# Scores of a step stand behind the values of the step two ahead, in an attention and MLP stack on one core

## The chip, the core and the metric

The program runs on one core of a Trainium2 chip. Its time is the device time in us of that core. Before the change it took 1929.63 us (median of three runs, 1927.41 to 1931.17). TensorE (PE in the rows) multiplies matrices, VectorE (DVE), ScalarE (ACT) and GpSimd (POOL) do elementwise work, and SyncE (SP) issues most DMAs. Each engine takes its own instructions in the order in which they are written and waits at semaphores for the others.

## The reference

256 tokens of width 1024 go through four layers of a first block and two layers of a second block.

```
first block, for each of 4 layers:
    q, k, v (and more) = x @ w_in
    mix = dsa | dilated | moba attention (by layer: 0 and 3, 1, 2)
    mo  = memory attention, 4 heads
    x = layer_norm(ALPHA * x + concat(mix, mo) @ w_out)
    x = layer_norm(ALPHA * x + (silu(x @ w_gate) * (x @ w_up)) @ w_down)
second block, for each of 2 layers:
    u = rms_norm(x) @ w_in
    differential, latent (MLA) and sliding window attention, each gated and projected
    x = x + rms_norm(y @ w_out);  x = x + sigmoid(x @ w_ple_gate) * (p @ w_ple_proj)
```

Every attention is scores, mask, softmax, values, in float32.

## The kernel before

**Weights.** Each weight matrix comes in units of two 128-row tiles by up to 512 columns. SP loads a unit into `raw` (ten slots), ScalarE rounds it to `w_hi` (L1205, eight slots), GpSimd makes the rest `w_lo` (L1177), and TensorE multiplies it for both token tiles, t 0 and t 1 (`products`, L1407 to L1414): three matmuls for each 128 rows, so six 128x512 matmuls for a unit and a token tile. A chunk is up to 512 output columns and accumulates in one bank of `acc` per token tile.

**Attention.** A `Step` treats two heads (three maps in the dilated attention of layer 1). Its work goes from engine to engine: scores on TensorE (`do_scores`, L1429) into banks of `acc`; logits on VectorE (L1911, or L1909), which frees the banks; row maxima (L1925); exponentials on ScalarE (L1255); the reciprocal of the sums on VectorE (`combine`, L1956); the normalisation, of the first map on GpSimd (L1188) and of the second on ScalarE (L1265); the transposes on TensorE (`turn`, L1447) into `tps`; the copy to `PT` on VectorE (L1968); and the values on TensorE (`do_values`, L1471, L1480) into `ops`. Then ScalarE and VectorE write the output as a high and a low part (L1285, L2005), which the products with `w_out` read. In the first block a layer has eight steps, 0 and 1 for the memory and 2 to 7 for the heads (layer 1 has six in all). The second block has four steps for each of its three attentions in each layer, 24 in all. Scores use two banks (2 and 3) in most layers, so the scores of a step wait until the logits of the one before have been read. The logits of a step are written over those of the third step before it.

**What sets the order.** `Plan` makes a list of tasks, each with an engine, a cost in ns, the tasks that it follows, and a priority; `arrange` (L313) places them one by one: of all tasks that are ready, the one that can begin first on its engine, and of equal ones that with the lower `prio`, then the older. The result is one list for each engine, and the program is written from these lists. A dependence between two tasks of the same engine therefore becomes a place in the list and no semaphore wait. `attention` (L484) adds the tasks of the steps. The products of the chunks that come later, the memory's keys and values for the next layer (`memory_products`) and the first products with `w_out` (`lin` at L751 to L757) can stand between the attention's tasks. A unit of `w_out` needs the outputs of certain steps: the last unit of a chunk (k 6, row 4 by `MIXED`) needs those of the layer's last steps.

Of the kernel before, what the change touches and what calls it, by code (L numbers as in the profile page):

```python
# [292 lines left out]
class Plan:  # L293
# [190 lines left out]
    def attention(self, steps, qk, score_banks, clear=()):  # L484

        for i, s in enumerate(steps):
            s.s, s.i = len(self.steps), i
            s.before = self.steps[-1] if self.steps else None
            s.before3 = self.steps[-3] if s.s >= 3 else None
            s.slot = s.s % 3  # L490
            size = s.width * s.maps
            s.at = 2 * CAUSAL * s.slot if size <= 2 * CAUSAL else 3 * CAUSAL * (s.s % 2)
            s.over = [e for e in self.steps[-4:] if e is s.before3 or
                      (e.at < s.at + size and s.at < e.at + e.width * e.maps)]
            self.steps.append(s)
            s.qk = qk[i] if isinstance(qk, dict) else qk
            b1, b3 = s.before, s.before3
            wide = s.width * s.maps
            s.scores = self.task("PE", "scores", s, 450 * s.maps, "scores_ready",
                                 [*s.qk, *s.apart, b1.scores if i else None], prio=0,  # L500
                                 room=("acc", s.banks or score_banks))
            after = [s.scores, s.mask_at]
            for e in s.over:
                after += [*e.turn[:e.turns], e.combine]
            s.logits = self.task("DVE", "logits", s, 160 + 1.03 * wide, "logits_ready", after, prio=0)
            s.scores.release = s.logits
            s.top = self.task("DVE", "maxima", s, 320 + 1.03 * wide + (1400 if s.flavour == "sinks" else 0),
                              "max_ready", [s.logits], prio=0)
            s.probs = self.task("ACT", "exponentials", s, 580 * s.maps + 0.83 * wide, "probs_ready", [s.top], prio=0)
            cost = {"differential": 400, "dilated": 1300, "sinks": 800}.get(s.flavour, 200)  # L510
            s.combine = self.task("DVE", "combine", s, cost, "combined",
                                  [s.probs, b3.outputs if b3 is not None else None], prio=0)
            for j in range(s.turns):
                done = s.probs
                if s.flavour == "differential":
                    done = s.mixed = self.task("DVE", "mix_maps", s, 700, "maps_mixed", [s.combine], prio=0)
                elif s.flipped:
                    on_pool = s.flavour != "dilated" and j == 0
                    s.normal[j] = self.task("POOL" if on_pool else "ACT", "normalise", (s, j),
                                            1000, "pool_normal" if on_pool else "act_normal", [s.combine], prio=0)  # L520
                    done = s.normal[j]
                blocks = 3 if s.width == CAUSAL else 4
                s.turn[j] = self.task("PE", "turn", (s, j), 110 * blocks, "t_ready", [done], prio=0,
                                      room=("tps", [(0,), (1,)]))
                s.take[j] = self.task("DVE", "take_turn", (s, j), 160 + 1.03 * P * blocks, "t_taken",
                                      [s.turn[j], b1.values if b1 is not None else None], prio=0)
                s.turn[j].release = s.take[j]
            s.values = self.task("PE", "values", s, 800, "pv_ready", [*s.take[:s.turns], *s.fed], prio=0,
                                 room=("ops", [(0,), (1,)]))
            if s.flipped:  # L530
                ready = s.values
                if s.block == 2:
                    ready = s.gated = self.task("DVE", "gate_output", s, 430, "out_gated", [s.values, *s.z_fed], prio=0)
                s.out_hi = self.task("ACT", "output_hi", s, 370 * len(s.out), "out_hi", [ready, *s.clear], prio=0)
                s.outputs = self.task("DVE", "outputs", s, 430 * len(s.out), "out_taken",
                                      [s.out_hi, b1.outputs if i else None], prio=0)
            elif s.flavour == "differential":
                s.outputs = self.task("DVE", "outputs", s, 1700, "out_taken", [s.values], prio=0)
            s.values.release = s.outputs
            for out in s.out if s.flipped else ():  # L540
                for t in range(T):
                    self.fed["mixed" if s.block == 1 else "s"][t][out[1]] = s.outputs
# [1528 lines left out]
```

How the kernel before makes its waits and increments, by code:

```python
        @block.sync  # L1116
# [1 line left out]
            def load_gain(g):  # L1118
                slot = g.slot
                if g.last is not None:
                    for done in g.last.rest:
                        sp.wait_ge(S["stage"], done.n)
                for done in g.apart:
                    sp.wait_ge(S[done.sem], done.n)
                name, row = g.g
                src = a[name] if row is None else a[name][row]
                to = Y[:, 0, :] if slot else gain[:, 0, :]
                sp.dma_start(to, src.partition_broadcast(P)).then_inc(gain_landed[slot], 16)
                if g.b[0]:
                    name, row = g.b
                    src = a[name] if row is None else a[name][row]
                    sp.dma_start(gain[:, 1, :], src.partition_broadcast(P)).then_inc(gain_landed[slot], 16)
# [1 line left out]
            def load_unit(u):  # L1134
                if u.u >= RAW:
                    sp.wait_ge(S["mm_done"], p.units[u.u - RAW].mm[1].n)
                ch = u.chunk
                src = u.weight[u.row * P:(u.row + u.nk) * P, ch.col:ch.col + ch.width]
                sp.dma_start(raw[:, u.u % RAW, 0:u.nk, 0:ch.width],
                             src.rearrange("(k p) n -> p k n", p=P)).then_inc(unit_landed[u.u % RAW], 16)
# [15 lines left out]
                elif k.kind == "save_rel_rows":  # L1157
                    n = P // REL_PIECES
                    sp.wait_ge(S["rel_rows_made"], 1)
                    sp.dma_start(rel_rows[:, n * k.it:n * k.it + n, :], rel_made.unsqueeze(1)
```

## Time and profile before

| | |
|---|---|
| median of 3 runs | 1929.63 us |
| profiled execution | 1926.78 us |
| its span | 1924.8 us |
| TensorE busy | 1870.4 us, 97% |
| GpSimd busy | 1523.6 us, 79% |
| ScalarE busy | 938.0 us, 49% |
| VectorE busy | 820.7 us, 43% |
| mean granted TensorE clock | 0.998 |

The span goes from the first to the last instruction of one profiled execution; the time of that execution is 2.0 us longer. Matmuls overlap in the pipeline, so a row's duration (0.39 us for 128x512) is longer than the distance from its start to that of the next (0.23 us). Where two rows follow each other without a wait, the distance of their starts is what the first one costs. The 54.4 us in which TensorE is not busy hold the start of the program, when no weights are there yet, and short waits. The weight loads of TensorE, PEld, run beside the matmuls.

### The profile page before, as it was taken

How to read it: one execution, taken by the hardware profiler on the slowest of the kernel's cores; microseconds unless marked ns; L12 is line 12 of the kernel's file. 1: busy time of each engine (PE TensorE's matmuls, PEld its weight loads, DVE VectorE, ACT ScalarE, POOL GpSimd, SP SyncE). 2: the span in 40 equal slices, each digit the busy share in tenths (PEclk: the TensorE clock that was granted, in tenths of full speed). 3: DMA queues.
4: the chain of work that ended last, by engine and by line, in shares of the span. 5: the costliest groups of instructions: out<-in, count | busy, mean ns of one | idle time of the engine just before them, and what ended most of it. 6: DMA issues, size and time to landing. Idle time of an engine off the chain costs nothing.

```text
span 1924.8 us, 27364 instructions
## 1 busy us (share of the span) xinstructions
PE 1870.4 (97%) x9610; PEld 1529.5 (79%) x9610; DVE 820.7 (43%) x1911; ACT 938.0 (49%) x1485; POOL 1523.6 (79%) x1332
## 2 busy tenths in 40 slices
PE   7999999999999999999999999999999999999998
PEld 6778888777888887788878678887887887788777
DVE  7774111346211255411047731106847436456534
ACT  4454444354444345444435644434656644556652
POOL 7858979885897977797977779797786887777785
PEclk9999999999999999999999999999999999999999
DMA  8444656564776554465645456655653555556453
GB/s 286 125 159 154 187 154 233 175 192 117 194 199 207 192 167 147 143 185 165 228 142 151 162 156 185 210 170 172 180 182 115 155 187 190 159 167 175 127 168 106
DMA packets 184269, 330.54 MB, mean 172 GB/s; under 512 B 12188, under 2 KB 44488, under 8 KB 184136
## 3 DMA queue, kind: packets, MB, share of 16 engines
q1 hardware_dynamic: 176224, 323.21, 53.9%
q10 hardware_dynamic: 7912, 5.59, 1.0%
q8 instruction: 80, 1.31, 0.3%
q14 instruction: 53, 0.43, 0.1%
HBM read 325.35 MB, written 3.41 MB: 171 GB/s over the span
## 4 chain that ended last, share of the span: by engine, by line
PE 83%; DVE 7%; POOL 5%; DMA 2%; issue 1%; ACT 1%; ACTq 0%; DVEq 0%
PE acc L1407 24%; PE acc L1408 23%; PE acc L1414 21%; POOL w_lo L1177 5%; PE tps L1354 4%; PE acc L1429 3%; PE ops L1471 2%; PE acc L1410 2%; PE tps L1447 2%; DMA raw<-in_w_down 1%; PE acc L1378 1%; PE acc L1380 1%; PE acc L1379 1%; PE ops L1366 1%; DVE small L1523 1%
## 5 line engine op out<-in xcount | busy, mean ns | idle before, releaser
L1177 POOL TENSOR_TENSOR w_lo<-raw,w_hi 128x512 fp32r<-128x512 f32 (+3 forms) x1244 | 1482.6, 1229 | 353.6 <-ACT w_hi L1205 352.3
L1205 ACT CAST w_hi<-raw 128x1024 fp32r<-128x1024 f32 (+3 forms) x624 | 615.4, 992 | 767.3 <-PE acc L1414 595.9
L1407 PE MATMUL acc<-w_hi,xT_hi 128*128 128x512 f32 (+1 forms) x1808 | 687.3, 384 | 12.4 <-ACT U L1235 3.0
L1408 PE MATMUL acc<-w_lo,xT_hi 128*128 128x512 f32 (+1 forms) x1808 | 666.9, 372 | 0.0
L1414 PE MATMUL acc<-w_hi,xT_lo 128*128 128x512 f32 (+2 forms) x1744 | 505.7, 371 | 0.0
L1407 PEld LDWEIGHTS acc<-w_hi,xT_hi 128*128 128x128 f32 x1808 | 341.6, 189 | 87.4 <-issue 19.5
L1408 PEld LDWEIGHTS acc<-w_lo,xT_hi 128*128 128x128 f32 x1808 | 342.1, 189 | 52.1
L1414 PEld LDWEIGHTS acc<-w_hi,xT_lo 128*128 128x128 f32 x1744 | 318.2, 189 | 58.2 <-DVE xT_lo L1684 1.0
L1744 DVE TENSOR_TENSOR H<-G,acc 128x512 f32<-128x512 f32 (+1 forms) x48 | 30.9, 644 | 333.9 <-PE acc L1414 333.9
L1407 PE MATMUL acc<-w_hi,hT_hi 128*128 128x512 f32 x352 | 139.5, 396 | 3.7 <-POOL w_lo L1177 3.6
L1408 PE MATMUL acc<-w_lo,hT_hi 128*128 128x512 f32 x352 | 137.2, 390 | 0.0
L1737 DVE SCALAR_TENSOR_TENSOR acc<-x_rows,acc 128x512 f32<-128x512 f32 x32 | 22.2, 695 | 218.8 <-PE acc L1414 192.8
L1414 PE MATMUL acc<-w_hi,hT_lo 128*128 128x512 f32 x352 | 108.5, 389 | 0.0
L1255 ACT ACTIVATE L<-L,neg_max 128x128 f32<-128x128 f32 (+2 forms) x208 | 96.2, 464 | 20.3 <-DVE neg_max L1925 17.5
L1407 PEld LDWEIGHTS acc<-w_hi,hT_hi 128*128 128x128 f32 x352 | 66.1, 188 | 21.7 <-issue 9.0
L1407 PE MATMUL acc<-w_hi,sT_hi 128*128 128x512 f32 (+1 forms) x200 | 79.4, 397 | 1.1 <-DVE MKV L1734 1.1
L1408 PE MATMUL acc<-w_lo,sT_hi 128*128 128x512 f32 (+1 forms) x200 | 77.4, 387 | 0.0
L1414 PEld LDWEIGHTS acc<-w_hi,hT_lo 128*128 128x128 f32 x352 | 66.1, 188 | 14.1
L1408 PEld LDWEIGHTS acc<-w_lo,hT_hi 128*128 128x128 f32 x352 | 66.1, 188 | 12.7
L1684 DVE TENSOR_TENSOR hT_lo<-tps,hT_hi 128x512 fp32r<-128x512 f32 (+1 forms) x48 | 31.1, 648 | 94.0 <-ACT hT_hi L1213 94.0
L1968 DVE COPY PT<-tps 128x384 f32<-128x384 f32 (+1 forms) x96 | 53.4, 574 | 38.2 <-PE tps L1447 33.8
L1188 POOL TENSOR_TENSOR L<-L,recips 128x128 f32<-128x128 f32 (+1 forms) x84 | 42.5, 528 | 32.8 <-DVE recips L1956 32.8
(207 smaller groups left out, 2010.0 us busy)
## 6 DMA issues: line engine op xcount, KB each, us to landing
raw<-in_w_gate_up SPq DMA_DIRECT2D x160, 512.0 KB, 4.0
raw<-in_w_in SPq DMA_DIRECT2D x104, 512.0 KB, 4.0
raw<-in_w_down SPq DMA_DIRECT2D x88, 512.0 KB, 3.7
raw<-in_w_out SPq DMA_DIRECT2D x48, 512.0 KB, 3.4
raw<-in_w_in_a SPq DMA_DIRECT2D x32, 512.0 KB, 3.6
raw<-in_w_in_b SPq DMA_DIRECT2D x20, 512.0 KB, 4.2
raw<-in_w_mem_kv SPq DMA_DIRECT2D x16, 512.0 KB, 4.2
raw<-in_w_gate_up SPq DMA_DIRECT2D x32, 256.0 KB, 2.8
```

The costliest lines, as they stand in the source:

```text
L1177: ins = nc.gpsimd.tensor_tensor(w_lo[:, r, i, 0:ch.width], raw[:, r, i, 0:ch.width], w_hi[:, slot, i, 0:ch.width].bitcast(F32), ALU.subtract)
L1188: ins = nc.gpsimd.tensor_tensor(part, part, by, ALU.mult)
L1205: nc.scalar.copy(w_hi[:, u.u % SPLIT, 0:u.nk, 0:u.chunk.width], raw[:, u.u % RAW, 0:u.nk, 0:u.chunk.width]).then_inc(S["hi_ready"], 1)
L1255: ins = nc.scalar.activation(part, part, ACT.Exp, bias=neg_max[:, slot, c:c + 1], accum_out=sums[:, slot, c:c + 1])
L1354: ins = nc.tensor.transpose(tps[0:width, k.slot[0], P * i:P * i + P], rows(src)[:, t, col:col + width], ident[:])
L1407: nc.tensor.matmul(o, hi[:, tok], wh, start=first_k, stop=False)
L1408: ins = nc.tensor.matmul(o, hi[:, tok], wl, start=False, stop=False)
L1410: ins = nc.tensor.matmul(o, lo[:, tok], wh, start=False, stop=last_k)
L1414: ins = nc.tensor.matmul(acc[:, bank, 0:ch.width], act_tile(ch.acts, u.k0 + i)[1][:, P * t:P * t + P], w_hi[:, u.u % SPLIT, i, 0:ch.width] ...
L1429: ins = nc.tensor.matmul(acc[:, k.slot[m], c], QT[base:base + n, qt, P * t:P * t + P], KT[kbase:kbase + n, kt, 0:c.stop - c.start], start= ...
L1447: ins = nc.tensor.transpose(tps[:, k.slot[0], P * i:P * i + P], lg[:, j, P * i:P * i + P], ident[:])
L1968: v.tensor_copy(PT[:, j, 0:blocks * P], tps[:, s.turn[j].slot[0], 0:blocks * P]).then_inc(S["t_taken"], 1)
```

## The change

The task of a step's scores follows one more task, the values of the step two ahead of it in the same attention, and its priority becomes -2 (it was 0, as for other attention tasks; products have 1 and 2). Nothing else is edited; all engines' orders are made anew from it.

```
@@ attention
             s.scores = self.task("PE", "scores", s, 450 * s.maps, "scores_ready",
-                                 [*s.qk, *s.apart, b1.scores if i else None], prio=0,
+                                 [*s.qk, *s.apart, b1.scores if i else None, steps[i - 2].values if i >= 2 else None], prio=-2,
                                  room=("acc", s.banks or score_banks))
```

First place, TensorE in layer 3, where the attention ends. L1471 are values, L1429 scores, L1447 transposes of `L`, L1407 to L1410 products of the first `w_out` chunk. Before, from the values of step 2:

```order
L1471 MATMUL ops<-PT,U 64x256
L1471 MATMUL ops<-PT,U 64x128
L1471 MATMUL ops<-PT,U 64x256
L1471 MATMUL ops<-PT,U 64x128
L1429 MATMUL acc<-KT,QT 128x128 x2
L1429 MATMUL acc<-KT,QT 128x256 x2
L1447 MATMUL tps<-ident,L 128x128 x6
L1471 MATMUL ops<-PT,U 64x256
L1471 MATMUL ops<-PT,U 64x128
L1471 MATMUL ops<-PT,U 64x256
L1471 MATMUL ops<-PT,U 64x128
L1447 MATMUL tps<-ident,L 128x128 x3
```

Now, with the values of step 4 in the middle:

```order
L1447 MATMUL tps<-ident,L 128x128 x9
L1471 MATMUL ops<-PT,U 64x256
L1471 MATMUL ops<-PT,U 64x128
L1471 MATMUL ops<-PT,U 64x256
L1471 MATMUL ops<-PT,U 64x128
L1429 MATMUL acc<-KT,QT 128x128 x2
L1429 MATMUL acc<-KT,QT 128x256 x2
L1447 MATMUL tps<-ident,L 128x128 x3
L1471 MATMUL ops<-PT,U 64x256
L1471 MATMUL ops<-PT,U 64x128
L1471 MATMUL ops<-PT,U 64x256
L1471 MATMUL ops<-PT,U 64x128
```

The scores in the first piece are those of step 6, which stood ahead of the values of steps 3, 4 and 5. In the second piece the scores of step 6 stand behind the values of step 4, and three sets of transposes, two of step 4 and one of step 5, stand ahead of those values.

Second place, TensorE in layer 0, at the values of the last step. Before (`mT` are the memory's activations, `w_out` products read `sT` and `xT`):

```order
L1447 MATMUL tps<-ident,L 128x128 x3
L1407 MATMUL acc<-w_hi,mT_hi 128x512
L1408 MATMUL acc<-w_lo,mT_hi 128x512
L1407 MATMUL acc<-w_hi,mT_hi 128x512
L1408 MATMUL acc<-w_lo,mT_hi 128x512
L1414 MATMUL acc<-w_hi,mT_lo 128x512 x2
L1471 MATMUL ops<-PT,U 64x256
L1471 MATMUL ops<-PT,U 64x128
L1471 MATMUL ops<-PT,U 64x256
L1471 MATMUL ops<-PT,U 64x128
L1407 MATMUL acc<-w_hi,mT_hi 128x512
L1408 MATMUL acc<-w_lo,mT_hi 128x512
```

Now:

```order
L1447 MATMUL tps<-ident,L 128x128 x9
L1471 MATMUL ops<-PT,U 64x256
L1471 MATMUL ops<-PT,U 64x128
L1471 MATMUL ops<-PT,U 64x256
L1471 MATMUL ops<-PT,U 64x128
L1447 MATMUL tps<-ident,L 128x128 x3
L1471 MATMUL ops<-PT,U 64x256
L1471 MATMUL ops<-PT,U 64x128
L1471 MATMUL ops<-PT,U 64x256
L1471 MATMUL ops<-PT,U 64x128
L1407 MATMUL acc<-w_hi,xT_hi 128x512
L1408 MATMUL acc<-w_lo,xT_hi 128x512
```

The products of the memory that stood between and behind the last values stand earlier now, and the `w_out` pair that reads the last step's output (`xT`) follows the last values at once.

Third place, TensorE in the second block, layer 0, differential attention, now (L1480 are its values, 128x416 and 128x512 the columns of other chunks):

```order
L1414 MATMUL acc<-w_hi,xT_lo 128x416 x2
L1480 MATMUL ops<-U,PT 128x128 x3
L1429 MATMUL acc<-KT,QT 128x128 x2
L1429 MATMUL acc<-KT,QT 128x256 x2
L1407 MATMUL acc<-w_hi,xT_hi 128x512
L1408 MATMUL acc<-w_lo,xT_hi 128x512
L1407 MATMUL acc<-w_hi,xT_hi 128x512
L1408 MATMUL acc<-w_lo,xT_hi 128x512
L1414 MATMUL acc<-w_hi,xT_lo 128x512 x2
L1407 MATMUL acc<-w_hi,xT_hi 128x416
L1408 MATMUL acc<-w_lo,xT_hi 128x416
L1407 MATMUL acc<-w_hi,xT_hi 128x416
```

Here the scores moved behind the values as well, and products of other chunks stand ahead of the next values and behind the scores.

## Rows read from the trace of the kernel before

**Rows 1.** The page, part 1: busy us, share of the span, instructions.
```profile
PE 1870.4 (97%) x9610; PEld 1529.5 (79%) x9610; DVE 820.7 (43%) x1911; ACT 938.0 (49%) x1485; POOL 1523.6 (79%) x1332
```

**Rows 2.** Waits: engine, line, waited for, us in total, times, longest.
```profile
ACT w_hi L1205 <- PE acc L1414: 595.9, 367, 6.1
```

**Rows 3.** Stretches: us, busy of PE, PEld, DVE, ACT, POOL; clock, DMA, GB/s.
```profile
119.00:149.00 30.00, 30.00 (x202) 21.78 (x202) 20.10 (x43) 22.83 (x72) 18.70 (x24) 1.00 0.31 106
...
1074.00:1102.00 28.00, 25.98 (x183) 18.21 (x182) 19.88 (x43) 23.69 (x73) 18.18 (x23) 1.00 0.38 123
1310.10:1313.30 3.20, 3.17 (x11) 2.68 (x11) 2.99 (x10) 2.02 (x3) 3.20 (x3) 0.50 0.25 93
```

**Rows 4.** Timeline of TensorE, attention ends: start, duration, line, tiles, shape, count, idle before.
```profile
119.24 0.93 PE L1429 MATMUL acc<-KT,QT 64*128 64x128 f32 x8
...
148.48 0.88 PE L1471 MATMUL ops<-PT,U 128*64 128x256 f32 x8
149.28 0.50 PE L1407 MATMUL acc<-w_hi,mT_hi 128*128 128x512 f32 x1
...
429.73 2.20 PE L1429 MATMUL acc<-KT,QT 64*128 64x128 f32 x12
...
460.87 1.61 PE L1471 MATMUL ops<-PT,U 128*128 128x256 f32 x8
...
774.08 0.88 PE L1471 MATMUL ops<-PT,U 128*64 128x256 f32 x8
...
1074.57 0.93 PE L1429 MATMUL acc<-KT,QT 64*128 64x128 f32 x8
...
1087.43 0.93 PE L1429 MATMUL acc<-KT,QT 64*128 64x128 f32 x8
...
1099.58 0.88 PE L1471 MATMUL ops<-PT,U 128*64 128x256 f32 x8
1101.57 0.50 PE L1407 MATMUL acc<-w_hi,xT_hi 128*128 128x512 f32 x1 [1.11 <-DVE xT_lo L2005]
```

**Rows 5.** Timeline of all engines, layer 2, the chain of step 4.
```profile
753.16 0.93 PE L1429 MATMUL acc<-KT,QT 64*128 64x128 f32 x8
...
754.21 0.96 DVE L1911 SCALAR_TENSOR_TENSOR L<-acc,masks 128x768 f32<-128x768 f32 x1 [1.48 <-PE acc L1429]
...
755.60 0.93 PE L1429 MATMUL acc<-KT,QT 64*128 64x128 f32 x8
...
756.25 0.40 ACT L1255 ACTIVATE L<-L,neg_max 128x128 f32<-128x128 f32 x1 [1.88 <-DVE neg_max L1925]
...
757.93 0.19 ACT L1255 ACTIVATION_READ_ACCUMULATOR L<-L,neg_max 128x1 f32 x1
...
758.81 0.97 POOL L1188 TENSOR_TENSOR L<-L,recips 128x128 f32<-128x128 f32 x2 [1.84 <-DVE recips L1956]
...
760.39 0.49 PE L1447 MATMUL tps<-ident,L 128*128 128x128 f32 x3
...
762.25 0.56 DVE L1968 COPY PT<-tps 128x384 f32<-128x384 f32 x1 [0.69 <-PE tps L1447]
...
763.54 0.88 PE L1471 MATMUL ops<-PT,U 128*64 128x256 f32 x8
```

**Rows 6.** Timeline of TensorE: products around scores, and scores behind values.
```profile
752.61 0.63 PE L1414 MATMUL acc<-w_hi,mT_lo 128*128 128x512 f32 x2
...
754.02 0.49 PE L1407 MATMUL acc<-w_hi,sT_hi 128*128 128x512 f32 x1
754.35 0.39 PE L1408 MATMUL acc<-w_lo,sT_hi 128*128 128x512 f32 x1
754.58 0.40 PE L1410 MATMUL acc<-w_hi,sT_lo 128*128 128x512 f32 x1
...
1082.66 0.88 PE L1471 MATMUL ops<-PT,U 128*64 128x256 f32 x8
1083.47 0.93 PE L1429 MATMUL acc<-KT,QT 64*128 64x128 f32 x8
```

More of the change, by code:

```diff
@@ L499, in attention @@
             s.scores = self.task("PE", "scores", s, 450 * s.maps, "scores_ready",
-                                 [*s.qk, *s.apart, b1.scores if i else None], prio=0,
+                                 [*s.qk, *s.apart, b1.scores if i else None, steps[i - 2].values if i >= 2 else None], prio=-2,
                                  room=("acc", s.banks or score_banks))
```

## The prediction

> Times are us. A step is one pass of attention over its heads; "step 4" is the fifth step of its layer, and S, T and V are its scores, its transposes ("turn") and its values on TensorE. A product pair is the six 128x512 matmuls of one weight unit for one token tile.
>
> **What bounds the kernel now.** I read the page's busy line first: TensorE is busy for 1870.4 of 1924.8 [rows 1], so whatever delays TensorE's queue costs time, unless other work fills the hole. Then the waits: ScalarE's weight split stands 595.9 behind products [rows 2]; it has its weights early and waits for buffers, so weight supply is not the bound. Third, the stretches. In layer 0's attention (119 to 149) TensorE is busy 30.00 of 30.00; in layer 3's (1074 to 1102) 25.98 of 28.00 [rows 3]. The present order hides the softmax chains even at the end of a layer's attention, where few products are left. Fourth, the rows of TensorE give the lengths of these ends: from S of step 3 to V of step 7 in layer 0, 119.24 to 148.48, 29.2; in layer 3, 1074.57 to 1099.58, 25.0; in layer 1 from S of step 3 to V of step 5, 429.73 to 460.87, 31.1; in layer 2 from S of step 4, 753.16, to V of step 7, 774.08, 20.9 [rows 4, 5]. Last, one chain with all engines, layer 2's step 4: 10.4 from S at 753.16 to V at 763.54 [rows 5].
>
> **What the change does.** No instruction is added or removed, and no semaphore wait. The edge and the priority enter the planner, which writes out the order of every engine. Before, up to four steps were between their scores and their values; now there are two, and S of step i stands behind V of step i-2. Scores that follow values at once are 25 in the new order and 4 in the old, of 54. Since TensorE takes its queue in order, the wait is real all the same: steps 3, 5 and 7 form one chain, and 2, 4 and 6 another. What stands behind a V that isn't ready (the next S, transposes, products) waits too, and then the split, its low part and the loads of the units further on.
>
> **What the chain costs.** In [rows 5] the parts are S 0.93; logits (0.96) and maxima on VectorE until 756.25; exponentials from there to 758.12; normalise on GpSimd 758.81 to 759.78, 0.69 after the exponentials because VectorE's reciprocal came behind the partner step's maxima; a transpose at 760.39, 0.6 behind products; the second copy to 762.81; V at 763.54, 0.7 behind products. Without these three holds (2.0 together) it is 8.4. With them it is 10.4. The longest that stands near a layer's end is 12.2, layer 3's step 7 (S at 1087.43 to V at 1099.58) [rows 4]. The partner step remains in the new order and TensorE's own queue is emptier there, so the price lies between 8.4 and 12.2; I take 10.4, the one row with a single partner just behind it.
>
> **The sum, layer by layer.** A V or an S takes its slot of 0.8 to 0.9, a product pair 6 x 0.23 = 1.4 [rows 6].
> Layer 3: the same work stands between S of step 3 and V of step 7 in both orders, four pairs of 512 columns with some of 256. Now three chains and two V: 3 x 10.4 + 1.6 = 32.8, against 25.0: +7.8.
> Layer 2: S of step 5 stands 2.4 behind S of step 4 [rows 5]. From there to its V the new order holds five pairs (6.8), two S (1.7), one V (0.8) and four transposes (0.3 each): 10.5. I take 11.3, since 27.1 of such slots took 29.2 in layer 0's old stretch. Then V 0.8 and step 7's chain 10.4: 24.9. One pair has moved in from behind: 24.9 - 20.9 - 1.4 = +2.6.
> Layer 0: from S of step 3 to V of step 5 the new order holds eleven pairs (15.0), four of half the columns (2.9), four S, three V and eight transposes (8.2): 26.1, taken as 28 in the same way, and more than two chains, so TensorE itself sets this part. Then V 0.8 and one chain: 39.2. Four pairs have moved in, 5.5: 39.2 - 29.2 - 5.5 = +4.5.
> Layer 1 (dilated steps; from S to V 16.4 to 18.3 in the trace): chain 16.4, then 2.9 of V and one pair before S of step 5, then about 15: 34.3 - 31.1 - 1.4 = +1.8, with 0 and +4 as bounds.
> Ends: the last pair of the first output chunk needs the last step's output. Layer 3 pays 1.11 for this already (the product at 1101.57), layer 0 has a ready memory pair behind V (149.28) [rows 4]. In the new order layers 0, 1 and 2 have nothing ready either: 3 x 1.1 = +3.3. Layers 0 and 1 then run the rest tile by tile as layers 2 and 3 do, and the layer norm is waited for a little longer: +1.5, by estimate between 0 and 2.2.
> The second block (24 steps) keeps products and gates of other branches between S and V: 0 there, and up to +2.
> Stalls together: 7.8 + 2.6 + 4.5 + 1.8 + 3.3 + 1.5 = +21.5.
>
> **What it gives back.** S uses 64 rows of the array, V 64 columns, products all of it. Two product matmuls before S take 0.55 instead of 0.46, and the first product after it 0.33 instead of 0.23 (754.02 to 754.35 to 754.58). V next to S is not dearer than V before a product: 1082.66 to 1083.47 is 0.81, 148.48 to 149.28 is 0.80 [rows 4, 6]. So a joined pair saves one entry and one exit, 0.19. There are 21 more; 8 of them stand in stretches where TensorE waits anyway. 13 x 0.19 = -2.5, bounds 0 and -4.0.
> The Trainium skill, TensorEngine Tiling (Array Packing), Key Properties, says that a change of tiling mode drains the engine; by it V next to S still changes mode, and standing adjacent removes one of the four boundaries at most. The trace agrees: V keeps its 0.81 before S. If the joined blocks shared one mode, the saving would be about twice as large, -5.
>
> **Clock.** The granted clock is 1.00 (2.4 GHz) in both stretches, and 0.50 (1.2 GHz) in two pieces of the whole trace, one of them at 1310.1 to 1313.3, where TensorE had waited for its inputs before [rows 3]. A piece loses half its length, 1.7, if TensorE has work. The new order makes ten or so stalls of 1 to 2.5 in layers 0, 2 and 3, with only S, T and V between them. I take two more pieces, +3, bounds 0 and +10.
>
> Sum: 21.5 - 2.5 + 3 = +22. The profiled execution took 1926.8 for its span of 1924.8; with it 1948.8. That execution lies 2.8 under the median of the runs, 1929.6, so the forecast is 1929.6 + 22 = 1951.6.
>
> **Rivals.**
> Short chains. If a chain in an emptier queue falls to 8.4, layer 3 is 3 x 8.4 + 1.6 = 26.8 (+1.8), layer 2 +0.6, layer 0 +2.5, layer 1 0, ends 3.3, and -2.5: about +6, 1936 (1929.6 + 6). For it: 2.0 of the 10.4 were holds. Against it: the partner step shares VectorE and ScalarE as it did there, and in the new order transposes of both steps stand in front of the first one's V.
> Slow clock and long chains. 12.2 a chain gives +13.2 in layer 3, +4.4, +6.3, +4 and 4.8 of ends, 33; even at 11 a chain (24.7) with six slow pieces (+10) and -2.5 it is +32, 1962. For it: the piece at 1310. Against it: the clock held at 1.00 through 1074 to 1102.
> Array changes decide (faster). If waits hide behind the moved pairs, only the 21 joins stay, 21 x 0.19 = -4.0: 1925.6. The point is in layer 3: two V and three chains must fit into 25.0, so a chain must be under (25.0 - 1.6) / 3 = 7.8. The bare parts add to 8.4, which speaks against it.
> The new order costs nothing: supply. If GpSimd, busy for 79% [rows 1], set the pace over a layer, a stall at its attention is caught up later in a faster run of products. Then 1929 to 1931. The 595.9 of [rows 2] says that ready buffers wait for TensorE, so there is nothing to catch up with.
>
> **Chances.** Forecast 0.68, short chains 0.13, slow clock and long chains 0.12, array changes 0.04, supply 0.03. About 0.2% (4) is what a measurement of this kernel tells from no change. Faster is the fourth, 0.04; same the fifth, 0.03; slower the rest, 0.93. The range goes from the short chains' 1936 to just past the slow clock's 1962: 1936 to 1966. It leaves out the two last rivals, part of the short chains and the far end of the long ones.
>
> **What the new profile would show.** Layer 3: V of step 7 about 33 behind S of step 3, with waits of 1 to 2.5 before T and V that end on VectorE's copies or on the normalise. Layer 0 and 2 with one such cycle each, and the product behind their last V about 1.1 late. The second block's stretches as long as before. TensorE's idle time in the waits up by some 20, its product groups' means unchanged. Joined S behind V at 0.81. A clock piece of 0.50 or two in layers 0 to 3. The prediction is wrong if layer 3's stretch stays under 28, if the chain from S to V is under 9 there, or if a stretch of the second block grows by more than 2.

## The result, and the profile after

The changed kernel takes 1957.2 us (median of four runs, 1954.7 to 1958.26) against 1930.4 for the kernel before beside it: ratio 1.0142, 95% interval 1.0127 to 1.0157. The forecast was 1951.6, with 1936 to 1966 as its range. The two profiled executions are further apart than the medians, 1926.8 and 1956.7; their spans differ by 29.9, and the rows below are held against that.

The page's busy line of the changed kernel, columns as in [rows 1]:

```profile
PE 1883.3 (96%) x9610; PEld 1538.6 (79%) x9610; DVE 815.3 (42%) x1911; ACT 943.5 (48%) x1489; POOL 1522.9 (78%) x1332
```

TensorE is busy for 12.9 longer than in [rows 1] with the same 9610 matmuls, and idle for 17.0 longer (71.4 against 54.4). The windows divide this between the blocks; the cut is a product in the MLP of layer 3. Columns as in [rows 3]. Kernel before:

```profile
0.00:1298.60 1298.60, 1268.35 (x6410) 1032.53 (x6411) 479.20 (x1121) 600.25 (x911) 1054.94 (x930) 1.00 0.57 177
1298.60:1924.70 626.10, 602.10 (x3201) 496.92 (x3200) 341.49 (x791) 337.73 (x574) 468.70 (x402) 0.99 0.52 160
```

Changed kernel:

```profile
0.00:1330.40 1330.40, 1281.33 (x6411) 1040.51 (x6412) 477.71 (x1121) 601.02 (x911) 1052.98 (x930) 0.99 0.56 173
1330.40:1954.70 624.30, 601.93 (x3201) 498.04 (x3199) 337.57 (x791) 342.45 (x578) 469.91 (x402) 0.99 0.53 161
```

The first block is 31.8 longer: 18.8 of idle time (30.3 to 49.1) and 13.0 of busy time. The second block is 1.8 shorter. Layer by layer, from the same matmuls in both orders: layer 0 +5.6, layer 1 +2.6, layer 2 +8.5, layer 3 +15.0. Two parts of this stand ahead of the ends of the attentions: 2.0 of layer 2's come before S of its step 4 (753.16 and 763.36 are 10.2 apart, the layer's start 8.2), and 2.5 of layer 3's before S of its step 3 (1074.57 and 1093.77 are 19.2 apart, the layer's start 16.7).

TensorE's waits in the changed kernel (waited for, us, times, longest):

```profile
PE ops L1471 <- DVE PT L1968: 9.4, 12, 1.7
PE ops L1480 <- DVE PT L1968: 6.1, 1, 6.1
PE tps L1354 <- DVE x_rows L1585: 5.0, 5, 1.7
...
PE tps L1447 <- ACT L L1265: 4.6, 4, 1.7
...
PE acc L1407 <- DVE xT_lo L2005: 2.8, 3, 0.9
...
PE tps L1447 <- POOL L L1188: 2.4, 5, 0.9
```

In the kernel before, the first five of these were 0.9, 0.3, 3.3, 0.7 and 1.1, and its list does not have the sixth. The waits are at the values (L1471, L1480), at the transposes of `L` (L1447), at the first product behind the last step (L1407), and at the layer norm (L1354). The row with a single wait of 6.1 is in the second block.

The end of layer 3's attention, TensorE alone, columns as in [rows 4]. It answers to the rows of layer 3 there, where S of step 3 to V of step 7 took 25.0:

```profile
1093.77 0.93 PE L1429 MATMUL acc<-KT,QT 64*128 64x128 f32 x8
...
1101.47 0.88 PE L1471 MATMUL ops<-PT,U 128*64 128x256 f32 x8 [0.88 <-DVE PT L1968]
1102.27 0.93 PE L1429 MATMUL acc<-KT,QT 64*128 64x128 f32 x8
...
1105.71 0.88 PE L1471 MATMUL ops<-PT,U 128*64 128x256 f32 x8 [1.70 <-DVE PT L1968]
1106.52 0.93 PE L1429 MATMUL acc<-KT,QT 64*128 64x128 f32 x8
...
1112.24 0.55 PE L1447 MATMUL tps<-ident,L 128*128 128x128 f32 x3 [1.72 <-ACT L L1265]
1113.33 0.87 PE L1447 MATMUL tps<-ident,L 128*128 128x128 f32 x6 [0.54 <-POOL L L1188]
1114.62 0.88 PE L1471 MATMUL ops<-PT,U 128*64 128x256 f32 x8 [0.41 <-DVE PT L1968]
...
1118.06 0.88 PE L1471 MATMUL ops<-PT,U 128*64 128x256 f32 x8 [1.24 <-DVE PT L1968]
1118.87 0.93 PE L1429 MATMUL acc<-KT,QT 64*128 64x128 f32 x8
...
1128.98 1.56 PE L1471 MATMUL ops<-PT,U 128*64 128x256 f32 x8 [0.78 <-DVE PT L1968]
1131.46 0.79 PE L1407 MATMUL acc<-w_hi,xT_hi 128*128 128x512 f32 x1 [0.92 <-DVE xT_lo L2005]
```

Read it as one chain: S of step 3 at 1093.77, its V at 1105.71, at once S of step 5, its V at 1118.06, at once S of step 7, its V at 1128.98. That is 11.9 + 0.8 + 11.5 + 0.8 + 10.1 = 35.2. The steps 4 and 6 form the other chain, 12.35 and 10.5 long.

Why a chain is longer than the 10.4 of [rows 5] is in the other engines' rows, for steps 4 and 5:

```profile
1104.89 7.46 POOL L1177 TENSOR_TENSOR w_lo<-raw,w_hi 128x512 fp32r<-128x512 f32 x6
...
1108.57 0.19 ACT L1255 ACTIVATION_READ_ACCUMULATOR L<-L,neg_max 128x1 f32 x1
1108.58 1.01 DVE L1925 TENSOR_REDUCE neg_max<-L 128x2 f32<-128x256 f32 x2
...
1109.51 0.17 DVE L1956 RECIPROCAL recips<-sums 128x4 f32<-128x4 f32 x1
1109.63 0.40 ACT L1255 ACTIVATE L<-L,neg_max 128x128 f32<-128x128 f32 x1 [0.87 <-DVE neg_max L1925]
...
1111.40 1.48 ACT L1265 ACTIVATE L<-L,recips 128x128 f32<-128x128 f32 x4
...
1112.31 1.89 POOL L1188 TENSOR_TENSOR L<-L,recips 128x128 f32<-128x128 f32 x4
```

Step 4's exponentials end at 1108.76 and its reciprocal at 1109.68. Its normalisation then stands behind step 5's exponentials on ScalarE (until 1111.40) and behind six pieces of weight splitting on GpSimd (until 1112.31). The two steps move side by side, so here each meets the other on VectorE and ScalarE.

The granted clock, in windows around that end and around the wait of 6.1:

```profile
1125.00:1137.00 12.00, 9.98 (x38) 6.80 (x37) 3.73 (x7) 1.91 (x4) 2.90 (x3) 0.57 0.37 113
...
1726.00:1734.00 8.00, 3.92 (x13) 3.42 (x14) 7.04 (x22) 1.12 (x1) 2.34 (x2) 0.57 0.23 63
```

Pieces at 0.50 (1.2 GHz) add up to 34.1 us in the changed kernel, in six places (784.8, 791.6, 1010.1, 1126.1, 1341.2, 1726.9), against 6.8 in two before; a last one, at the end of each program, where TensorE has no more work, is left out. Three of the six are at the ends of the attentions of layers 2 and 3, and one begins inside the wait of 6.1. The one at 1341.2 answers to the one at 1310 before. The one at 1010.1 stands behind a layer norm, where TensorE waits 1.70 and 0.77 in both kernels; in the two runs below that leave the first block's order as it was and change the second block alone, a piece of 3.4 stands at this place too (at 995.6 and 994.5), so it is not shown to come from the change.

The clock is not the luck of one execution: it was 0.991 or 0.992 over each of the four runs of the changed kernel, and 0.993 to 0.999 over the 38 runs of the kernel before that stand beside the experiments, with medians of 0.996 and 0.997. By an estimate from these, 0.005 of 1957, the slow clock makes up to 10 of the 26.8 us between the medians.

### The profile page after: what moved, and what is told of

It is laid out like the page before. It is cut to its first block, busy times and chain, and to the rows that moved or that the text cites. A ratio compares the mean times of both kernels' runs of the same rounds, so it can differ in the third digit from the quotient of the medians.

```text
span 1954.7 us, 27369 instructions
## 1 busy us (share of the span) xinstructions
PE 1883.3 (96%) x9610; PEld 1538.6 (79%) x9610; DVE 815.3 (42%) x1911; ACT 943.5 (48%) x1489; POOL 1522.9 (78%) x1332
## 4 chain that ended last, share of the span: by engine, by line
PE 80%; DVE 9%; POOL 6%; issue 2%; DMA 2%; ACT 1%; ACTq 0%; DVEq 0%
PE acc L1407 23%; PE acc L1408 22%; PE acc L1414 21%; POOL w_lo L1177 6%; PE tps L1354 4%; PE acc L1429 3%; PE ops L1471 2%; PE acc L1410 1%; PE tps L1447 1%; DMA raw<-in_w_down 1%; DVE small L1523 1%; PE ops L1366 1%; PE acc L1378 1%; PE acc L1380 1%; PE acc L1379 1%
## 5 line engine op out<-in xcount | busy, mean ns | idle before, releaser
L1205 ACT CAST w_hi<-raw 128x1024 fp32r<-128x1024 f32 (+3 forms) x624 | 616.3, 992 | 754.8 <-PE acc L1414 579.9
L1407 PE MATMUL acc<-w_hi,xT_hi 128*128 128x512 f32 (+1 forms) x1808 | 688.8, 385 | 11.9 <-DVE xT_lo L2005 2.8
L1407 PEld LDWEIGHTS acc<-w_hi,xT_hi 128*128 128x128 f32 x1808 | 342.5, 189 | 86.9 <-issue 16.8
L1407 PE MATMUL acc<-w_hi,hT_hi 128*128 128x512 f32 x352 | 139.6, 397 | 3.4 <-POOL w_lo L1177 3.2
L1255 ACT ACTIVATE L<-L,neg_max 128x128 f32<-128x128 f32 (+2 forms) x208 | 96.2, 464 | 35.4 <-DVE neg_max L1925 30.3
L1407 PEld LDWEIGHTS acc<-w_hi,hT_hi 128*128 128x128 f32 x352 | 66.1, 188 | 21.4 <-issue 8.7
L1407 PE MATMUL acc<-w_hi,sT_hi 128*128 128x512 f32 (+1 forms) x200 | 80.5, 402 | 1.0 <-DVE U L1700 0.5
L1968 DVE COPY PT<-tps 128x384 f32<-128x384 f32 (+1 forms) x96 | 53.1, 574 | 35.2 <-PE tps L1447 29.3
```

Of the source, the lines that this page charges most:

```text
L1205: nc.scalar.copy(w_hi[:, u.u % SPLIT, 0:u.nk, 0:u.chunk.width], raw[:, u.u % RAW, 0:u.nk, 0:u.chunk.width]).then_inc(S["hi_ready"], 1)
L1255: ins = nc.scalar.activation(part, part, ACT.Exp, bias=neg_max[:, slot, c:c + 1], accum_out=sums[:, slot, c:c + 1])
L1407: nc.tensor.matmul(o, hi[:, tok], wh, start=first_k, stop=False)
L1968: v.tensor_copy(PT[:, j, 0:blocks * P], tps[:, s.turn[j].slot[0], 0:blocks * P]).then_inc(S["t_taken"], 1)
```

## Experiments

Every ratio is against runs of the kernel before that were taken beside the experiment on the same chip. It comes with its 95% interval and need not be the quotient of the two medians. Differences between two versions that were not taken side by side are read from their ratios.

**The dependence alone.** Priority left at 0.

```
-  [*s.qk, *s.apart, b1.scores if i else None], prio=0,
+  [*s.qk, *s.apart, b1.scores if i else None, steps[i - 2].values if i >= 2 else None], prio=0,
```

> The scores follow the values of the step two ahead, the priority stays 0. Theory A (the chains of softmax at the ends of the first block's attentions): the dependence does it alone, so +22 to +29 us against the kernel before. Theory B (the priority pulls scores ahead of other work and hurts): under +8 us here.

1957.82 us, ratio 1.0148 (1.0119 to 1.0178). The dependence does all of it.

**The priority alone.** `prio=-2` without the dependence.

> Priority -2 for scores, no new dependence. Theory A: within 4 us of the kernel before, since as many steps are in flight as before. Theory B: +15 us or more.

1932.18 us, ratio 1.0019 (1.0006 to 1.0033): a small loss, if one.

**The change in the second block alone.** The condition is `i >= 2 and s.block == 2`, and the priority is -2 only there.

> The whole change, but only for the 24 steps of the second block, where products stand between a step's scores and values. Theory A: -3 to +2 us: joins of scores behind values give up to 2.5 us, the waits are hidden. Theory C (the stall of 6.0 us at the values of the last differential step in the second layer of this block, behind a VectorE stage that GpSimd slows, belongs to the change and not to its neighbours): +3 to +8 us, with that stall in the trace.

1928.46 us, ratio 0.9994 (0.9977 to 1.0011). Its trace has the same wait of 6.1 at L1480, and no net loss all the same.

**The change in the first block alone.** The same with `s.block == 1`.

> The whole change, but only for the steps of the first block. Theory A: nearly all of it, +25 to +30 us, with layer 3 the largest share (15 us in the changed kernel's trace, slow clock pieces included). If the loss were spread over all 54 steps: +15 us.

1961.42 us, ratio 1.0155 (1.013 to 1.0181). The whole loss is in the first block.

**Layer 3 alone.** `22 <= s.s < 30` are its eight steps.

```
+  ..., steps[i - 2].values if i >= 2 and 22 <= s.s < 30 else None], prio=-2 if 22 <= s.s < 30 else 0,
```

> The edge and the priority only for the eight steps of layer 3 of the first block. Theory (each layer's stalls add up, in the stretch where few products are left): layer 3 grows by about as much as in the changed kernel, S of step 3 to V of step 7 takes 34 to 35 instead of 25.0, and the whole by 11 to 15 with one slow clock piece, ratio 1.006 to 1.008. Rival (the loss is made by the state in which the layers ahead leave the buffers and the weights): less than 6, ratio under 1.003, and chains near 10.4 instead of 11 to 12.

1941.57 us, ratio 1.0062 (1.0042 to 1.0082). The span is 14.0 longer than before's, of which 13.8 are there when the second block's first values come. The stretch from S of step 3 to V of step 7, TensorE busy first:

```profile
1075.10:1111.20 36.10, 26.34 (x172) 18.39 (x171) 19.53 (x41) 23.58 (x72) 23.83 (x27) 0.95 0.31 103
```

36.1 instead of 25.0, with 9.8 idle and a slow piece of 3.4 inside. The waits are those of the changed kernel, to the hundredth at most places: 0.88 and 1.70 ahead of the first two V, 1.72 ahead of a transpose. So the loss of layer 3 is made where it shows and not handed on by the layers ahead: 13.8 alone, and 12.5 from S of step 3 on in the changed kernel.

**Row maxima computed twice in the first block, in both orders.** Each step's row maxima (L1925) are reduced a second time, which adds about 1.0 on VectorE to every chain; results are the same.

```
-  for t in range(T):
+  for n, t in enumerate([*range(T), *range(T)] if s.block == 1 else range(T)):
```

In the changed kernel:

> The changed kernel; the row maxima of the first block's steps are computed twice, 1.0 us more on VectorE in each of 30 chains. Theory A (chains in series set the ends of the attentions): layer 3's stretch grows by 3, layer 2's by 1 to 2, layer 0's by 1 to 2, layer 1's by 1 to 2, so +5 to +9 us on the changed kernel, some +33 to +37 against the kernel before. If TensorE's queue and not the chain sets these ends: under +2 on the changed kernel.

In the kernel before:

> The kernel before with the same doubled maxima in the first block. Theory A: four steps in flight hide most of it, 0 to +3 us against the kernel before, in layer 3 above all. If the old order was as near to its chains as the new one: +5 to +9 us.

1973.01 us, ratio 1.0239 (1.0217 to 1.0261), for the new order, 16 to 19 more than the changed kernel by medians and by ratios; 1943.58 us, ratio 1.0074 (1.006 to 1.0087), for the old, 14 more than before. Both are misses. In the new order 5 to 9 more were expected. Its four runs go from 1965.58 to 1979.55 while their clock falls from 0.992 to 0.984, so a part of the 16 is slow clock, and only the quickest run (the profiled one) lies in what was expected. The old order was expected to hide the extra work and lose 3 at most. Layer 3's stretch from S of step 3 to V of step 7 grows by 4.0 there, from 25.0 to 29.0 (VectorE's busy time is the third):

```profile
1087.00:1116.00 29.00, 24.62 (x172) 17.34 (x170) 24.70 (x54) 22.10 (x71) 15.19 (x21) 1.00 0.34 110
```

VectorE is busy for 24.70 of 29.00, against 19.88 of 28.00 in [rows 3], and TensorE for 24.62. That would fit a stretch which, with up to four steps in flight, VectorE's sum of work sets and not one chain; it is not shown, since TensorE waits 2.5 for VectorE's copies there too. The pair of runs doesn't tell a latency limit from a throughput limit. It shows that the old order had almost no room for 1.0 more on VectorE in each step either.

**Filler matmuls, heavy and light.** In steps 4 to 7 of layers 0, 2 and 3 of the changed kernel, extra 128x128 matmuls whose output nobody reads stand ahead of the waits. Heavy: three ahead of each transpose wait and four ahead of each V; the wait for a free slot of `tps` moves ahead of them. Light: two ahead of each V only, as shown.

```
+  if s.block == 1 and s.flavour == "plain" and s.i >= 4:
+      for i in range(2):
+          nc.tensor.matmul(ops[:, slot, 384:512], ident[:], ident[:], start=True, stop=True)
   pe.wait_ge(S["t_taken"], max(g.n for g in s.take[:s.turns]))
```

> The changed kernel with idle TensorE time filled: before the wait for the normalised probabilities three matmuls of the identity with itself, before the wait for the copies four, in steps 4 to 7 of layers 0, 2 and 3 (their results are not used). If the slow clock pieces at 785 to 795 and 1126 to 1136 come from these stalls and cost time: both go, and the kernel gains 3 to 6 us on the changed one (+21 to +25 against the kernel before). If they cost nothing because TensorE waits anyway: the pieces go and the time stays within 1.5. If the filler itself delays the chain: slower, with a full clock.

> The changed kernel with two extra 128x128 matmuls ahead of the wait of each V in steps 4 to 7 of layers 0, 2 and 3 (24 in all, about 0.2 each, written to a part of the bank that V overwrites or nobody reads). Theory (the slow clock pieces come from the thin work in the stalls and cost about half their length): some of the pieces near 785 and 1126 go, and the time falls by 2 to 5 against the changed kernel, ratio 1.011 to 1.013. Rival (the clock pieces cost nothing there because TensorE waits anyway, and the filler only adds to the chain): the same or up to 5 slower, ratio 1.014 to 1.017, whether or not the pieces go.

Heavy: 1969.27 us, ratio 1.0211 (1.0198 to 1.0225). The slow pieces near 790 and 1126 are gone, but the filler lengthened the chains (layer 3's stretch is 37.6 for 35.2), so its time prices nothing. Light: 1953.91 us, ratio 1.0138 (1.0107 to 1.017), which can't be told from the changed kernel's 1.0142, so what the filler gains as a whole is not shown. In its trace the pieces near 790 and 1126 are gone too, and one of 3.4 is left at 1017.6 behind the layer norm. What a slow piece costs can be read from the same work in both traces, from the product behind the last V to the first transposes of the layer norm. Changed kernel, layer 0, and the end of the piece in layer 3 (it starts at 1131.46, shown above):

```profile
159.00 0.50 PE L1407 MATMUL acc<-w_hi,xT_hi 128*128 128x512 f32 x1 [0.92 <-DVE xT_lo L2005]
...
172.88 0.63 PE L1354 MATMUL tps<-ident,x_rows 128*128 128x128 f32 x4
...
1147.61 0.63 PE L1354 MATMUL tps<-ident,x_rows 128*128 128x128 f32 x4
```

Light filler, layer 3:

```profile
1136.01 0.50 PE L1407 MATMUL acc<-w_hi,xT_hi 128*128 128x512 f32 x1 [0.94 <-DVE xT_lo L2008]
...
1149.88 0.63 PE L1354 MATMUL tps<-ident,x_rows 128*128 128x128 f32 x4
```

With the clock at 1.00 this piece takes 13.9, in layer 0 of the changed kernel and in layer 3 with the filler (13.87). In layer 3 of the changed kernel it starts at 1131.46 inside a slow piece that ends at 1136.4, and takes 16.15. So 4.9 of slow clock cost 2.3, just under a half. The same work in layer 2 takes 15.45 in the changed kernel, with 3.4 of slow clock in it, and 13.9 with the filler. The Trainium skill, TensorE: Matmul & The Clock Gate, Terms, puts the penalty of slow time at that time x (1 - K/N), which is half at 1.2 GHz; the rows agree, where TensorE has work all the time.

The saving didn't reach the profiled span, 1962.0. That execution had another wait, at the program's start, and a slow piece (6.8, at 41) behind it:

```profile
PE tps L1354 <- DVE QT L1588: 9.5, 3, 8.6
```

The changed kernel's trace doesn't have this wait of 8.6; the execution of the dependence alone has one like it. What brings it is open.

**The wait of 6.1 in the second block.** VectorE and GpSimd in the changed kernel around it:

```profile
1718.14 10.20 POOL L1177 TENSOR_TENSOR w_lo<-raw,w_hi 128x512 fp32r<-128x512 f32 x8 [4.03 <-ACT w_hi L1205]
...
1721.00 1.22 DVE L1530 SCALAR_TENSOR_TENSOR small<-small 128x4 f32<-128x4 f32 x1
...
1727.18 1.18 DVE L1533 SCALAR_TENSOR_TENSOR small<-small 128x4 f32<-128x4 f32 x1
1728.40 0.16 DVE L1534 SCALAR_TENSOR_TENSOR small<-small 128x4 f32<-128x4 f32 x1
...
1729.38 0.56 DVE L1968 COPY PT<-tps 128x384 f32<-128x384 f32 x1
...
1730.08 1.62 PE L1480 MATMUL ops<-U,PT 128*128 128x128 f32 x6 [6.05 <-DVE PT L1968]
```

In the new order the stage `latent_scale` (a square root by steps on 128x4 numbers, L1529 to L1535) stands ahead of the copy that step 45's values need. Its operations take 1.2 each while GpSimd splits weights, and 0.16 from the moment GpSimd ends, at 1728.3. In the kernel before, the stage of this layer stands behind that copy, and GpSimd's row of 1689.17 ends at 1690.5 and its next begins at 1695.0:

```profile
1689.68 0.56 DVE L1968 COPY PT<-tps 128x384 f32<-128x384 f32 x1
...
1691.55 0.16 DVE L1530 SCALAR_TENSOR_TENSOR small<-small 128x4 f32<-128x4 f32 x1
```

Two experiments put the stage behind that copy, first with the change in the second block alone, then with the whole change:

```
-  scale = p.task("DVE", "stage", Stage("latent_scale", ...), 3400, None, bq.take)
+  scale = p.task("DVE", "stage", Stage("latent_scale", ...), 3400, None,
+                 [*bq.take, *([steps[-1].take[0]] if l == 1 else [])])
```

> The change for the second block's steps alone, and in its layer 1 the VectorE stage latent_scale (eleven operations of 4 columns, up to 1.2 us each beside GpSimd) is placed behind the copy of the last differential step's transposes. If that stage is the cause of the 6.0 us wait at the last differential values, the wait goes and the kernel gains 4 to 7 us on the version without this edit, so -4 to -7 against the kernel before. If something else holds these values, no change: -1 to +1.

> The full change, and in layer 1 of the second block the stage latent_scale stands behind the first copy of the last step's transposes. Theory (the second block's part of the change is a stall of 6.1 at the values of step 45, behind VectorE's small operations that a burst on GpSimd makes slow, and the slow clock after it): the wait of L1480 on the copy L1968 goes, and the time falls by 6 to 9 against the changed kernel, to a ratio of 1.010 to 1.011 against the kernel before. Rival (the stall was only where waiting for supply or for GpSimd became visible, and turns up at another line): less than 3 saved, ratio 1.013 or more.

Second block alone: 1924.25 us (1922.09 to 1925.8), ratio 0.9966 (0.9952 to 0.9981), against 0.9994 (0.9977 to 1.0011) without the move. This version beats both kernels by a little; against the one without the move the intervals just touch. Whole change: 1955.53 us, ratio 1.0123 (1.0093 to 1.0152), by medians and ratios 2 to 4 less than the changed kernel instead of the 6 to 9 expected, and not clear of noise. Its profiled execution has a slow piece of 10.2 at 154.8, at the end of layer 0's attention, which the changed kernel's trace doesn't have although the order there is the same. The theory of this wait was half right. The wait at L1480 is gone in both, but a new one stands at the transposes of the stage's own output (waits of the whole change with the move):

```profile
PE tps L1355 <- DVE U L1854: 4.5, 1, 4.5
```

It was 0.2 before the move. Counted from S of step 42, step 45's values come 7.6 earlier, and 5.6 of that is given back by the values of step 49. Most of the expected gain turned into this wait, which is what the rival had described.

## Why the prediction was right, and which terms were off

**What bounds the kernel.** Right. ScalarE still waits for buffers behind products, 579.9 us in the changed kernel against the 595.9 of [rows 2], so supply never took over and nothing lost in the first block was caught up.

**Layer 3.** Right in place and kind, short in size: 35.2 for the predicted 32.8. The price of a chain, taken as 10.4 from the one row of [rows 5], was 10.1 to 12.35, with 11.3 as the mean of five. In the rows of steps 4 and 5 it is the partner's exponentials and the weight split that stand in front of the normalisation. The bound 8.4 to 12.2 held but for 0.15. The price was picked low. Of the old order's chains from step 3 on in layers 0, 2 and 3, the one of [rows 5] is the shortest; the others take 11.6 to 15.3. Nor was 12.2 the longest near a layer's end: step 5 of layer 3 goes from 1079.94 to 1093.16, 13.2. The waits ahead of T and V are up to 1.7, several of them under 1, where 1 to 2.5 was forecast. The rest of layer 3's 15.0 is slow clock: 2.5 ahead of the attention, at the piece of 1010, and 2.3 behind it.

**Layers 0, 1 and 2.** Layer 0 took 5.6 for 4.5 + 1.1 of the end: right, with a stretch of 38.3 for 39.2. Layer 1 took 2.6 for 1.8 + 1.1: right in total, but its parts were not. Its stretch is 33.1 for 34.3, no wait for `xT_lo` stands behind it, and two waits that were not there before, 0.8 and 0.7, stand at its layer norm and behind it. The prediction's range of its chains, 16.4 to 18.3, leaves out step 4, from 433.55 to 456.60, 23.05. Layer 2 took 8.5 for 2.6 + 1.1, the largest miss by layer. 2.0 of it come ahead of S of step 4, in steps 0 to 3, for which the sum had no term. The stretch from S of step 4 to V of step 7 is 26.2 for 24.9, with the slow piece at 784.8 in it. Behind it 0.9 is the wait of the end, and 1.5 the slow piece at 791.6, by the comparison with the filler above.

**Ends.** The product behind the last V waits 0.9 for `xT_lo` in layers 0, 2 and 3; 1.1 was taken, for layers 0, 1 and 2 in addition to what layer 3 paid. The layer norm took 1.7 in two more waits (3.3 to 5.0 at L1354); 1.5 was taken.

**Stalls together.** 21.5 was forecast for TensorE's added idle time in the first block, 18.8 came. So the terms for waiting add up to a little more than came, and what is missing from the sum is busy time.

**Array changes.** V next to S kept its 0.80 (1101.47 to 1102.27 above). The saving of 2.5 can't be seen. In the second block 12 scores follow values at once where 3 did, and with the wait at L1480 taken out TensorE's busy time is 1871.5 against 1870.4. TensorE was busy for 11.3 of that execution's slow clock, against 6.8 before; half of the difference is 2.2, which leaves -1.1 for nine joined pairs. The change in the second block alone with the wait left in, which has the same joined pairs, leaves +0.7 by the same working. So a saving of 0.19 for each pair is neither shown nor ruled out.

**The clock.** This is the term that was wrong: two pieces and +3 were taken, 27.3 us more of slow clock came, and busy time rose by 12.9. TensorE was busy for 28.3 of the slow clock in the changed kernel and for 6.8 of it before; by the half shown above this costs 10.7, so the clock explains most of the 12.9 and 2 stay open. The bound of +10 was at its edge. The mechanism was named rightly (stalls of 1 to 2.5 with only S, T and V between) for three of the pieces, which both fillers removed; the count was not. I went by the piece of 3.4 at 1310 [rows 3] and took each as short as that, while the one at 1126 lasts 10.2.

**The second block.** Right on the sum (-1.8, and 0.9994 alone), wrong on the way. I expected its stretches to stay as they were. They grow and shrink as products change sides: from S of step 42 to V of step 45 it is 43.1 for 31.4, with 48 more matmuls in it, and the last attention of that layer is 7.5 shorter. In the first of these stands the wait of 6.1, which I had not looked for because I followed TensorE's order and not VectorE's. By the test that the prediction set itself (a stretch of the second block more than 2 longer) this step fell. It cost nothing in sum since other waits of the block went: those of L1378 and L1407 for ScalarE's `tmp` and `U`, 3.9 and 3.0 before, are 0 and 0.2. The version at 0.9966 fits that: in its profiled execution TensorE is idle for 3.0 less than before and busy for 1.1 more.

**Rivals.** Short chains are out (no chain in layer 3 under 10.1). "Slow clock and long chains", to which I gave 0.12, describes what happened better than the forecast does. It asked for 11 a chain and +10 of clock and put 1962 on this; the chains of layer 3 are 11.3 in the mean, the clock cost about 10.7, and 1957.2 lies a little nearer to 1962 than to 1951.6. Between the two profiled executions the difference is 29.9, for its +32 and the forecast's +22. That the forecast came as near as it did is in part luck: stalls were taken 2.7 too high for the first block and a saving was subtracted that no trace shows, while the clock was short by 8 to 10. The range covered both mechanisms. No gain by array changes is shown; the best version, 0.9966, gains idle time in its profiled execution. The order that the planner made before hid these chains in the first block by keeping up to four steps in flight: chains of 11.6 to 13.2 in layer 3, with 2.0 idle in 28.0 [rows 3].

What stays open: why a slow piece lasts 3.4 in one place and 10.2 in another, why one execution has a piece at 154.8 and another of the same order there has none, and what the change would cost with no slow clock at all; the fillers removed pieces in two layers, and no run removed all.

## What to carry to other kernels

A dependence between two tasks of one engine that costs no semaphore can still set the pace: it limits how many chains are in flight, and where filler runs out the chain's length is what the engine takes. Price such a stall twice, as idle time and as the slow clock behind it; here busy time rose by 13.0 in the first block beside 18.8 more of idle time. Take the price of a chain from all its rows and not from one: the one taken here was the shortest. After a reorder by a planner, read the order of each engine that feeds the waiting one. The one large stall that was new stood in VectorE's order.

## What the runs showed of the hardware that was not expected

An operation of VectorE on 128x4 numbers in SBUF takes 0.16 alone and mostly 1.2 beside a run of GpSimd's elementwise work in SBUF, whose own eight operations take 10.20, 1.28 each. That is about one of VectorE's operations for each one of GpSimd's. In the kernel before, the same stage in layer 0 of the second block takes 1.2 an operation too (1388 to 1396), beside GpSimd and at a place where nobody waits for it. A twin of this stage keeps one of its two inputs in `ops`, in PSUM, and is not slowed by a run of GpSimd. In the run of the whole change with the moved stage:

```profile
1732.40 2.53 POOL L1178 TENSOR_TENSOR w_lo<-raw,w_hi 128x512 fp32r<-128x512 f32 x2 [2.20 <-ACT w_hi L1206]
...
1733.09 0.17 DVE L1543 SCALAR_TENSOR_TENSOR ops<-ops,small 128x8 f32<-128x8 f32 x1
```

The Trainium skill, SBUF — State Buffer, section "SBUF: two separate sides", calls the port pair that VectorE and GpSimd share an exclusive lock, held for a whole instruction, which an operation of VectorE with two SBUF inputs needs against a GpSimd operation that reads SBUF. The rows of both stages agree with that. One row of the first stage is not of this kind: its integer operation (L1531) has one tensor input and takes 1.22 as well; no run here shows why.
